# RMS norms of a two-layer hybrid block: squares on two engines, column sums in four column groups, and the inverse root worked out token by token

## The chip, the cores and the metric

The kernel runs on one core of a Trainium2 chip. Every time is device time in microseconds (us) of one launch, and the number to be predicted is its median over several runs. An engine is named as the profile names it: PE is TensorE's matmul, PEld its weight load, ACT ScalarE, DVE VectorE, POOL GpSimd, SP the engine that issues most DMAs.

## The reference, cut to what matters

```python
def rms_norm(x, g):
    xf = x.astype(jnp.float32)
    y = xf * lax.rsqrt(jnp.mean(xf * xf, axis=-1, keepdims=True) + RMS_EPS)
    return (y * g.astype(jnp.float32)).astype(x.dtype)

def modulate(h, shift, scale):
    return h * (1.0 + scale) + shift
...
for layer in range(DEPTH):                    # DEPTH = 2
    hc = modulate(rms_norm(cs, g_norm1), ...)   # 256 context tokens x 1024
    hx = modulate(rms_norm(x, g_norm1), ...)    # 256 latent tokens x 1024
    ... three mixers of h @ w_in, merged and projected: x_mid, c_mid ...
    hx2 = modulate(rms_norm(x_mid, g_norm2), ...)
    x_new = x_mid + gate * swiglu(hx2, w_ffn_in, w_ffn_out)
    # the context half of the second part is left out in the last layer
```

So there are four norms over the stream: three over 512 tokens (context and latent), and the last over the 256 latent tokens alone. Each ends in a large matrix product.

## The kernel before

The stream `X` lies in SBUF transposed: 128 partitions, `DT` = 8 tiles of channels (k), `TOK` = 512 tokens along the free axis. A norm must therefore sum squares across partitions and over the eight tiles, for each token.

The program is a row of stages. Each is one block in which every engine has its own instruction list and waits on counted signals; at a stage's end all engines meet, so nothing of the next stage starts earlier. In a stage each engine works strictly in the written order. `norm` is such a stage, called four times.

In it, in order of the work:

- ACT squares the eight tiles of `X` into `sq` (L614). Then it makes the high parts of the first three chunks of the next stage's weights (`high_ahead`, L615, the instruction is L327; 128x1024 each): weights are cut into a high and a low part so that three fp32r products give nearly an fp32 one.
- PE adds the squares up with a matrix of ones as weights, one fp32 product of 128x512 for each tile, all into bank 0 (L628). An fp32 product shows as two matmul records, so eight products are 16 records. Since `ones` is 128x128, every partition of bank 0 gets the sum.
- DVE makes the three low parts (`low_ahead`, L644, the instruction is L330), then waits for the sums, scales them and adds epsilon (L646, 128x512), and takes the reciprocal (L648, 128x512). ACT takes the square root (L617, 128x512). `rms` holds the inverse root for each token on all partitions.
- Then come the cells: one cell is one channel tile by one segment of 256 tokens, 16 cells in a norm over 512 tokens and 8 in the last. For each, DVE multiplies `X`, a scale and `rms` (L656), ACT adds the shift and rounds to the high part (L621), and the low part is made three cells later by DVE (L663) or, for every third cell, by POOL in two steps (L673, L675).
- PE waits for both segments of a channel tile and multiplies them with the first two weight tiles of the next stage (`AHEAD_TILES` = 2): six fp32r products for each k, 48 in all, into banks 0 and 1 (or 0 and 2). They are the last work of the stage.

In the two norms that open a layer SP also stores the result to DRAM at the end (`save`). The weight ring's first three loads for the next stage are issued in the stage before the norm.

Of the kernel before, what the change touches and what calls it, by code (L numbers as in the profile page):

```python
# [22 lines left out]
ACT = mybir.ActivationFunctionType  # L23
ALU = mybir.AluOpType
AX = mybir.AxisListType

P = 128
D = 1024
DT = D // P
SEQ = 256  # L30
CTX = 256
TOK = CTX + SEQ
# [26 lines left out]
RMS_EPS = 1e-6  # L59
# [9 lines left out]
CHUNKS = 3  # L69
# [110 lines left out]
def build_in(ctx, nc, ins, out):  # L180
    def sb(name, shape):
        return ctx.enter_context(nc.sbuf_tensor(name, shape, FP32))

    def sig(name):
        return Signal(ctx, nc, name)


    X = sb("X", [P, DT, TOK])
    ident = sb("ident", [P, P])
    ones = sb("ones", [P, P])  # L190
# [21 lines left out]
    BANK = ctx.enter_context(nc.psum_tensor("BANK", [P, 8, 512], FP32))  # L212
# [20 lines left out]
    WORK = place("WORK", WORK0, WORK_N)  # L233
# [3 lines left out]
    def carve(mem, at, *shape):  # L237
        n = 1
        for s in shape:
            n *= s  # L240
        flat = mem[:, at:at + n]
        if len(shape) == 1:
            return flat
        names = "abcd"[:len(shape)]
        return flat.rearrange(f"p ({' '.join(names)}) -> p {' '.join(names)}",
                              **{k: s for k, s in zip(names[1:], shape[1:])})
# [131 lines left out]
    pe_sig, act_sig, dve_sig, pool_sig = sig("pe_step"), sig("act_step"), sig("dve_step"), sig("pool_step")  # L378
    rows_turned = sig("rows_turned")
    turned_out = sig("turned_out")  # L380
    squares = sig("squares")
    sums = sig("sums")
    inverse_rms = sig("inverse_rms")
    scaled = sig("scaled")
# [6 lines left out]
    high_ready = sig("weights_high")  # L391
# [23 lines left out]
    class Modulation:  # L415
# [28 lines left out]
        def sums(self, a):  # L444

            return BANK[:, self.turned_bank, 32 * self.supers[a]:32 * (self.supers[a] + 1)]
# [157 lines left out]
    def norm(scale, shift, t0, ahead, banks, save=False):  # L604
        n = TOK - t0
        sq = carve(WORK, 0, DT, TOK)
        rms = carve(WORK, DT * TOK, TOK)
        segs = [s for s in range(2) if s * CTX >= t0]
        cells = [(k, s) for k in range(DT) for s in segs]
        with stage() as block:  # L610
            @block.scalar
            def _(act):
                for k in range(DT):
                    squares.mark(nc.scalar.activation(sq[:, k, t0:], X[:, k, t0:], ACT.Square))  # L614
                ahead.high_ahead(act)  # L615
                act.wait_ge(*dve_sig(2))
                inverse_rms.mark(nc.scalar.activation(rms[:, t0:], rms[:, t0:], ACT.Sqrt))  # L617
                for i, (k, s) in enumerate(cells):
                    a, b = s * CTX, (s + 1) * CTX
                    act.wait_ge(*scaled(i + 1))  # L620
                    gate_ready.mark(nc.scalar.activation(HS[0][:, k, a:b], sq[:, k, a:b], ACT.Identity, bias=shift[:, k, s:s + 1]))  # L621


            @block.tensor
            def _(pe):
                for k in range(DT):
                    pe.wait_ge(*squares(k + 1))
                    last = nc.tensor.matmul(BANK[:, 0, 0:n], ones[:], sq[:, k, t0:], start=(k == 0), stop=(k == DT - 1))  # L628
                sums.mark(last)

                weights = [(ahead.part(0, c), ahead.part(1, c)) for c in range(AHEAD_TILES)]
                pe.wait_ge(*low_ready(AHEAD_TILES))
                for k in range(DT):
                    i = len(segs) * (k + 1)
                    pe.wait_ge(*gate_ready(i))
                    pe.wait_ge(*h_ready(i - i // 3))
                    if i // 3:
                        pe.wait_ge(*evacuated(i // 3))
                    for w, bank in zip(weights, banks):
                        product3(BANK[:, bank, 0:n], [x[:, k] for x in w], [x[:, k, t0:] for x in HS], k == 0, k == DT - 1)  # L640

            @block.vector
            def _(dve):
                ahead.low_ahead(dve)  # L644
                dve.wait_ge(*sums(1))
                dve_sig.mark(nc.vector.tensor_scalar(rms[:, t0:], BANK[:, 0, 0:n], 1.0 / D, RMS_EPS, ALU.mult, ALU.add))  # L646
                dve.wait_ge(*dve_sig(1))
                dve_sig.mark(nc.vector.reciprocal(rms[:, t0:], rms[:, t0:]))  # L648
                dve.wait_ge(*inverse_rms(1))
                LAG = 3  # L650
                lows = [i for i in range(len(cells)) if i % 3 != 2]
                for i in range(len(cells) + LAG):
                    if i < len(cells):
                        k, s = cells[i]
                        a, b = s * CTX, (s + 1) * CTX
                        scaled.mark(nc.vector.scalar_tensor_tensor(sq[:, k, a:b], X[:, k, a:b], scale[:, k, s:s + 1],  # L656
                                                                   rms[:, a:b], ALU.mult, ALU.mult))
                    if i >= LAG and i - LAG in lows:

                        k, s = cells[i - LAG]  # L660
                        a, b = s * CTX, (s + 1) * CTX
                        dve.wait_ge(*gate_ready(i - LAG + 1))
                        h_ready.mark(nc.vector.scalar_tensor_tensor(HS[1][:, k, a:b], sq[:, k, a:b], shift[:, k, s:s + 1],  # L663
                                                                    HS[0][:, k, a:b].bitcast(FP32), ALU.add, ALU.subtract))

            @block.gpsimd
            def _(pool):
                for i, (k, s) in enumerate(cells):
                    if i % 3 == 2:

                        a, b = s * CTX, (s + 1) * CTX
                        pool.wait_ge(*gate_ready(i + 1))
                        pool_sig.mark(nc.gpsimd.tensor_scalar(sq[:, k, a:b], sq[:, k, a:b], shift[:, k, s:s + 1], None, ALU.add))  # L673
                        pool.wait_ge(*pool_sig(i // 3 + 1))
                        evacuated.mark(nc.gpsimd.tensor_tensor(HS[1][:, k, a:b], sq[:, k, a:b], HS[0][:, k, a:b].bitcast(FP32), ALU.subtract))  # L675

            @block.sync
            def _(sp):
                if save:

                    sp.wait_ge(*h_ready(len(cells) - len(cells) // 3))
                    sp.wait_ge(*evacuated(len(cells) // 3))
                    for x in range(2):
                        sp.dma_start(H_DRAM[x], HS[x].bitcast(FP32).rearrange("p k t -> p (k t)")).then_inc(h_saved, 16)
        ahead.early = CHUNKS
        Signal.end_stage()
# [1534 lines left out]
    for l in range(DEPTH):  # L2221
        t0 = CTX if l == DEPTH - 1 else 0
# [61 lines left out]
```

## Time and profile before

| what | value |
|---|---|
| median of 3 runs | 2302.93 us (2298.18 to 2304.2) |
| the profiled execution | 2312.29 us |
| its span (first to last instruction) | 2310.5 us |
| mean granted TensorE clock | 0.940 of full speed |
| PE busy | 2027.9 us (88%) |
| DVE busy | 1071.6 us (46%) |
| ACT busy | 775.8 us (34%) |
| POOL busy | 299.9 us (13%) |

The profiled execution is longer than its span by 1.8 us, and 9.4 us above the median of the runs. The busy shares are means over stages that have different limits; for a change to one kind of stage, only that stage's own timeline tells what bounds it. The granted clock is given as a share of 2.4 GHz: 1.00 is that, 0.50 is 1.2 GHz.

### The profile page before, as it was taken

The numbers are of one execution on the slowest core, as the hardware profiler recorded it, in microseconds if no ns is written. First come the engines' busy times: TensorE is split into PE (matmuls) and PEld (weight loads), VectorE is DVE, ScalarE is ACT, GpSimd is POOL, SyncE is SP. The second block draws the span as 40 slices with busy tenths as digits, with TensorE's granted clock in tenths as the row PEclk, the third lists the DMA queues.
The fourth block names the chain that finished last, engine by engine and source line by source line (L and its number), as shares of the span: only waits on it lengthen the run. The fifth ranks groups of instructions, "written<-read, shape, count | busy, mean of one in ns | idle before, by whom it ended". The sixth has DMA issues, their size and how long they took to land. (4 is left out here: it accounts for less than half of the span.)

```text
span 2310.5 us, 51557 instructions
## 1 busy us (share of the span) xinstructions
PE 2027.9 (88%) x22759; PEld 1596.8 (69%) x22759; DVE 1071.6 (46%) x1753; ACT 775.8 (34%) x1419; POOL 299.9 (13%) x380
## 2 busy tenths in 40 slices
PE   4886888879989998989998998968886998988998
PEld 2662877643567887678886665737775457988988
DVE  1635666652643333353332216476666254545544
ACT  1433333223432222232221114253332343434432
POOL 1102333202000111010001001043331110100000
PEclk8997999989989999999999998979998999999999
DMA  7416000120111332223326753100003012654543
GB/s 269 146 64 237 5 4 5 37 108 1 37 58 62 102 92 83 73 76 107 102 81 235 281 172 123 33 1 4 4 5 123 21 37 94 183 166 135 184 152 123
DMA packets 144606, 220.75 MB, mean 96 GB/s; under 512 B 6846, under 2 KB 123800, under 8 KB 137216
## 3 DMA queue, kind: packets, MB, share of 16 engines
q1 hardware_dynamic: 142880, 215.74, 27.5%
q8 instruction: 181, 2.97, 0.5%
q0 software_dynamic: 1504, 1.71, 0.2%
q14 instruction: 41, 0.34, 0.0%
HBM read 208.00 MB, written 9.44 MB: 94 GB/s over the span
## 5 line engine op out<-in xcount | busy, mean ns | idle before, releaser
L366 PE MATMUL BANK<-H_high,W_high 128*128 128x512 f32 (+2 forms) x1472 | 524.3, 356 | 70.8 <-ACT H_high L621 32.3
L330 DVE TENSOR_TENSOR W_low<-RING,W_high 128x1024 fp32r<-128x1024 f32 x268 | 328.0, 1232 | 466.6 <-ACT W_high L327 466.5
L367 PE MATMUL BANK<-H_low,W_high 128*128 128x512 f32 (+2 forms) x1472 | 519.5, 353 | 0.0
L368 PE MATMUL BANK<-H_high,W_low 128*128 128x512 f32 (+2 forms) x1472 | 518.9, 353 | 0.0
L327 ACT ACTIVATE W_high<-RING 128x1024 fp32r<-128x1024 f32 x268 | 279.2, 1052 | 618.1 <-PE BANK L368 585.1
L366 PEld LDWEIGHTS BANK<-H_high,W_high 128*128 128x128 f32 (+1 forms) x1472 | 283.7, 193 | 118.0 <-issue 50.7
L367 PEld LDWEIGHTS BANK<-H_low,W_high 128*128 128x128 f32 (+1 forms) x1472 | 284.1, 193 | 37.8 <-issue 1.1
L368 PEld LDWEIGHTS BANK<-H_high,W_low 128*128 128x128 f32 (+1 forms) x1472 | 283.3, 192 | 37.7
L1231 PE MATMUL BANK<-RING,WORK 64*64 64x64 f32 x4480 | 177.6, 225 | 11.4 <-issue 6.1
L1231 PEld LDWEIGHTS BANK<-RING,WORK 64*64 64x64 f32 x4480 | 154.4, 137 | 25.3 <-issue 9.3
L1042 POOL TENSOR_TENSOR WORK<-WORK,masks 128x256 f32<-128x256 f32 x160 | 122.8, 781 | 250.5 <-ACT WORK L1083 151.6
L1231 PE MATMUL BANK<-WORK,RING 64*64 64x64 f32 x3072 | 133.6, 232 | 15.5 <-issue 12.7
L366 PE MATMUL BANK<-hidden_high,W_high 128*128 128x512 f32 (+1 forms) x352 | 123.3, 350 | 12.0 <-PEq L2051 12.0
L1231 PE MATMUL BANK<-RING 64*64 64x64 f32 (+1 forms) x2944 | 102.3, 257 | 30.3 <-DVE RING L1137 20.9
L1231 PEld LDWEIGHTS BANK<-WORK,RING 64*64 64x64 f32 x3072 | 112.8, 142 | 20.5 <-issue 16.6
L367 PE MATMUL BANK<-hidden_low,W_high 128*128 128x512 f32 (+1 forms) x352 | 120.9, 343 | 0.0
L368 PE MATMUL BANK<-hidden_high,W_low 128*128 128x512 f32 (+1 forms) x352 | 120.8, 343 | 0.0
L1231 PEld LDWEIGHTS BANK<-RING 64*64 64x64 f32 x2944 | 94.9, 150 | 33.9 <-issue 31.4
L1172 DVE TENSOR_TENSOR RING<-RING,BANK 128x512 f32<-128x512 f32 x128 | 83.8, 684 | 62.6 <-PE BANK L1231 60.4
L1091 ACT ACTIVATE WORK<-BANK 128x256 f32<-128x256 f32 (+1 forms) x160 | 58.0, 363 | 119.3 <-PE BANK L1231 105.3
L1989 POOL TENSOR_TENSOR merge_tiles<-merge_tiles 128x512 f32<-128x512 f32 (+1 forms) x32 | 33.7, 1063 | 481.7 <-DVE merge_tiles L1971 481.7
L366 PEld LDWEIGHTS BANK<-hidden_high,W_high 128*128 128x128 f32 x352 | 68.0, 193 | 34.8 <-issue 27.7
(270 smaller groups left out, 2904.3 us busy)
## 6 DMA issues: line engine op xcount, KB each, us to landing
modulation_weights<-w_mod_dram SPq DMA_DIRECT2D x48, 1024.0 KB, 6.5
RING<-w_in_dram SPq DMA_DIRECT2D x46, 1024.0 KB, 5.7
RING<-w_ffn_in_dram SPq DMA_DIRECT2D x44, 1024.0 KB, 5.2
RING<-w_ffn_out_dram SPq DMA_DIRECT2D x20, 1024.0 KB, 5.5
RING<-w_out_dram SPq DMA_DIRECT2D x8, 1024.0 KB, 5.3
h_high<-H_high SPq DMA_DIRECT2D x2, 2048.0 KB, 6.5
h_low<-H_low SPq DMA_DIRECT2D x2, 2048.0 KB, 12.6
H_high<-h_high SPq DMA_DIRECT2D x2, 2048.0 KB, 12.2
```

Of the source, the lines that this page charges most:

```text
L327: high_ready.mark(nc.scalar.activation(self.part(0, c), self.raw(c), ACT.Copy))
L330: low_ready.mark(nc.vector.tensor_tensor(self.part(1, c), self.raw(c), self.part(0, c).bitcast(FP32), ALU.subtract))
L366: nc.tensor.matmul(out, w[0], x[0], start=start, stop=False)
L367: nc.tensor.matmul(out, w[0], x[1], start=False, stop=False)
L368: return nc.tensor.matmul(out, w[1], x[0], start=False, stop=stop)
L1042: s_lm[d].mark(nc.gpsimd.tensor_tensor(LM[d], LTS[d], lanes(level_mask(d, l)), ALU.mult))
L1091: s_x1_out[d].mark(nc.scalar.activation(X1[d][:, :, cols], pairs(4 * d + B_L, 0)[:, :, cols], ACT.Copy))
L1172: s_t[d].mark(nc.vector.tensor_tensor(T2[d].rearrange("p q j t -> p q (j t)"), T2[d].rearrange("p q j t -> p q (j t)"), BANK[:, 4 * d + B_ ...
L1231: last[x] = nc.tensor.matmul(BANK[to[h], bank, at + j * width:at + (j + 1) * width], lhs(j)[rows[h]], rhs(j)[rows[h]], start=start and (j ...
L1989: pool_sig.mark(nc.gpsimd.tensor_tensor(total(m), total(m), gate(u), ALU.add))
```

## The change

The squares of the even tiles stay on ACT, those of the odd tiles go to DVE. PE adds tile k into column group k mod 4 of bank 0, with weights of only 32 columns: four groups of 32 partitions, each holding the sum of two tiles. ACT copies that bank to SBUF (`partial`). PE then multiplies each block of 128 tokens of `partial`, as weights, with one column of ones: token by token, 128 partitions by 4 columns (2 in the last norm), in bank 6. DVE scales and inverts these 128x4 numbers, ACT takes their root, and PE spreads them back: weights are a column of `by_token` repeated 128 times, the moving matrix is the unit matrix, and the result, the inverse root of every token on all partitions, is left in bank 7. The cells read it there.

The making of the three weight parts ahead is spread between these steps: ACT makes the first high part after its squares, the second after the copy, the third after the root; DVE makes the first low part before the sums by token, the second and third after the reciprocal, and only then waits for bank 7.

```diff
-        rms = carve(WORK, DT * TOK, TOK)
+        partial = carve(WORK, DT * TOK, TOK)
+        by_token = carve(WORK, (DT + 1) * TOK, 4)
+        T_BANK, R_BANK = 6, 7
+        own = slice(t0 // P, TOK // P)
+        tiles = range(t0 // P, TOK // P)
...
             def _(act):
-                for k in range(DT):
+                for k in range(0, DT, 2):
                     squares.mark(nc.scalar.activation(sq[:, k, t0:], X[:, k, t0:], ACT.Square))
-                ahead.high_ahead(act)
+                ahead.make_high(act, 0)
+                act.wait_ge(*sums(1))
+                partial_kept.mark(nc.scalar.activation(partial[:, t0:], BANK[:, 0, 0:n], ACT.Copy))
+                ahead.make_high(act, 1)
                 act.wait_ge(*dve_sig(2))
-                inverse_rms.mark(nc.scalar.activation(rms[:, t0:], rms[:, t0:], ACT.Sqrt))
+                inverse_rms.mark(nc.scalar.activation(by_token[:, own], by_token[:, own], ACT.Sqrt))
+                ahead.make_high(act, 2)
...
             def _(pe):
                 for k in range(DT):
-                    pe.wait_ge(*squares(k + 1))
-                    last = nc.tensor.matmul(BANK[:, 0, 0:n], ones[:], sq[:, k, t0:], start=(k == 0), stop=(k == DT - 1))
+                    pe.wait_ge(*(odd_squares if k % 2 else squares)(k // 2 + 1))
+                    c = k % 4
+                    last = nc.tensor.matmul(BANK[32 * c:32 * (c + 1), 0, 0:n], ones[:, 0:32], sq[:, k, t0:], start=(k < 4), stop=(k >= DT - 4))
+                sums.mark(last)
+                pe.wait_ge(*partial_kept(1))
+                for t in tiles:
+                    last = nc.tensor.matmul(BANK[:, T_BANK, t:t + 1], partial[:, t * P:(t + 1) * P], ones[:, 0:1], start=True, stop=True)
+                sums.mark(last)
+                pe.wait_ge(*inverse_rms(1))
+                for t in tiles:
+                    last = nc.tensor.matmul(BANK[:, R_BANK, t * P:(t + 1) * P], by_token[:, t:t + 1].to_broadcast([P, P]), ident[:], start=True, stop=True)
                 sums.mark(last)
...
             def _(dve):
-                ahead.low_ahead(dve)
-                dve.wait_ge(*sums(1))
-                dve_sig.mark(nc.vector.tensor_scalar(rms[:, t0:], BANK[:, 0, 0:n], 1.0 / D, RMS_EPS, ALU.mult, ALU.add))
+                for k in range(1, DT, 2):
+                    odd_squares.mark(nc.vector.tensor_tensor(sq[:, k, t0:], X[:, k, t0:], X[:, k, t0:], ALU.mult))
+                dve.wait_ge(*high_ready(1))
+                ahead.make_low(0)
+                dve.wait_ge(*sums(2))
+                dve_sig.mark(nc.vector.tensor_scalar(by_token[:, own], BANK[:, T_BANK, own], 1.0 / (32 * D), RMS_EPS, ALU.mult, ALU.add))
                 dve.wait_ge(*dve_sig(1))
-                dve_sig.mark(nc.vector.reciprocal(rms[:, t0:], rms[:, t0:]))
-                dve.wait_ge(*inverse_rms(1))
+                dve_sig.mark(nc.vector.reciprocal(by_token[:, own], by_token[:, own]))
+                for c in range(1, CHUNKS):
+                    dve.wait_ge(*high_ready(c + 1))
+                    ahead.make_low(c)
+                dve.wait_ge(*sums(3))
...
                         scaled.mark(nc.vector.scalar_tensor_tensor(sq[:, k, a:b], X[:, k, a:b], scale[:, k, s:s + 1],
-                                                                   rms[:, a:b], ALU.mult, ALU.mult))
+                                                                   BANK[:, R_BANK, a:b], ALU.mult, ALU.mult))
```

## Rows read from the trace of the kernel before

**Rows 1.** The page, part 1: busy time, share, instructions of each engine.

```profile
PE 2027.9 (88%) x22759; PEld 1596.8 (69%) x22759; DVE 1071.6 (46%) x1753; ACT 775.8 (34%) x1419; POOL 299.9 (13%) x380
```

**Rows 2.** Timeline, first norm: start, duration (us), engine, line, operation, [idle before <-releaser].

```profile
54.03 4.26 ACT L614 ACTIVATE WORK<-X 128x512 f32<-128x512 f32 x8 [11.39 <-PEq L537]
...
58.20 2.93 ACT L327 ACTIVATE W_high<-RING 128x1024 fp32r<-128x1024 f32 x3
...
59.27 3.50 DVE L330 TENSOR_TENSOR W_low<-RING,W_high 128x1024 fp32r<-128x1024 f32 x3 [14.06 <-ACT W_high L327]
...
61.15 1.28 ACT L617 ACT_TABLE_LOAD   x1
...
63.35 0.69 DVE L646 TENSOR_SCALAR WORK<-BANK 128x512 f32<-128x512 f32 x1 [0.58 <-PE BANK L628]
64.08 3.35 DVE L648 RECIPROCAL WORK<-WORK 128x512 f32<-128x512 f32 x1
67.46 0.63 ACT L617 ACTIVATE WORK<-WORK 128x512 f32<-128x512 f32 x1 [5.03 <-DVE WORK L648]
68.13 1.67 DVE L656 SCALAR_TENSOR_TENSOR WORK<-X,scale,WORK 128x256 f32<-128x256 f32 x4 [0.70 <-ACT WORK L617]
```

**Rows 3.** Timeline of PE: the column sums of the first, second and last norm.

```profile
54.71 8.60 PE L628 MATMUL BANK<-WORK,ones 128*128 128x512 f32 x16 [10.15 <-ACT WORK L614]
...
972.84 7.13 PE L628 MATMUL BANK<-WORK,ones 128*128 128x512 f32 x16 [1.89 <-ACT WORK L614]
...
2089.57 3.72 PE L628 MATMUL BANK<-WORK,ones 128*128 128x256 f32 x16 [1.29 <-ACT WORK L614]
```

**Rows 4.** Timelines of ACT and DVE, second and last norm: first square, first cell.

```profile
972.15 4.26 ACT L614 ACTIVATE WORK<-X 128x512 f32<-128x512 f32 x8 [16.84 <-PEq L2007]
...
985.58 1.67 DVE L656 SCALAR_TENSOR_TENSOR WORK<-X,scale,WORK 128x256 f32<-128x256 f32 x4 [0.70 <-ACT WORK L617]
...
2089.10 2.56 ACT L614 ACTIVATE WORK<-X 128x256 f32<-128x256 f32 x8 [8.36 <-PEq L2007]
...
2098.73 1.68 DVE L656 SCALAR_TENSOR_TENSOR WORK<-X,scale,WORK 128x256 f32<-128x256 f32 x4 [0.48 <-ACT WORK L617]
```

**Rows 5.** Timeline of PE, first norm: first and last product of the tiles ahead.

```profile
71.27 0.77 PE L366 MATMUL BANK<-H_high,W_high 128*128 128x512 f32 x1 [7.96 <-ACT H_high L621]
...
84.07 0.39 PE L368 MATMUL BANK<-H_high,W_low 128*128 128x512 f32 x1
```

**Rows 6.** Stretches of the first norm: length, PE, PEld, DVE, ACT, POOL busy, PEclk, DMA.

```profile
54.00:58.00 4.00, 3.29 (x4) 1.50 (x5) 0.00 (x0) 3.97 (x8) 0.00 (x0) 0.54 0.00 0
...
71.00:75.00 4.00, 3.73 (x9) 3.00 (x10) 4.00 (x8) 1.93 (x5) 2.81 (x4) 0.53 0.00 0
```

**Rows 7.** Timeline of PE: products in four column groups of 32, elsewhere in the kernel.

```profile
31.27 1.06 PE L440 MATMUL BANK<-modulation_weights,condition_padded 128*32 128x512 f32 x8
...
37.50 1.94 PE L440 MATMUL BANK<-modulation_weights,condition_padded 128*32 128x512 f32 x8 [3.45 <-DMA modulation_weights<-w_mod_dram]
```

**Rows 8.** Timeline of PE: short fp32 products with 128x128 weights.

```profile
26.78 4.55 PE L574 MATMUL BANK<-ident,WORK 128*128 128x128 f32 x24
...
1391.32 1.03 PE L456 MATMUL BANK<-ident,modulation_rows 128*128 128x8 f32 x8 [0.76 <-DVE mod L479]
1392.72 1.85 PE L456 MATMUL BANK<-ident,modulation_rows 128*128 128x8 f32 x8 [0.38 <-DVE mod L479]
```

**Rows 9.** Groups by form: xcount | busy us, mean ns of one | idle before.

```profile
L656 DVE SCALAR_TENSOR_TENSOR WORK<-X,scale,WORK 128x256 f32<-128x256 f32 x56 | 28.0, 536 | 2.6 <-ACT WORK L617 2.6
...
L663 DVE SCALAR_TENSOR_TENSOR H_low<-WORK,mod,H_high 128x256 fp32r<-128x256 f32 x39 | 24.2, 636 | 0.0
...
L1997 DVE SCALAR_TENSOR_TENSOR X<-BANK,mod,X 128x256 f32<-128x256 f32 x48 | 20.6, 479 | 68.2 <-PE BANK L368 68.2
...
L1759 DVE RECIPROCAL WORK<-WORK 128x1 f32<-128x1 f32 x48 | 7.4, 154 | 0.9 <-ACT WORK L1787 0.2
...
L1105 ACT ACTIVATE decay<-WORK 128x4 f32<-128x4 f32 x32 | 6.3, 196 | 0.0
```

More of the change, by code:

```diff
@@ L380, in build_in @@
     turned_out = sig("turned_out")
-    squares = sig("squares")
+    squares, odd_squares, partial_kept = sig("squares"), sig("squares_of_odd_tiles"), sig("partial_sums_kept")
     sums = sig("sums")
```

## The prediction

> **What bounds the kernel now.** I read the page first: PE is busy 88% of the span [rows 1], so most stages are bound by products. That says nothing of a norm, so I read the timeline of each one. In the first, ACT's first square starts at 54.03 and DVE's first cell at 68.13: 14.1 us in which no cell is made [rows 2]. The reader should follow who ends last at each step. ACT's eight squares are over by 58.3, but PE adds them up one after another until 63.31 [rows 2, 3]; DVE has made its three low parts by 62.8 and waits 0.58 us for PE; then scale (0.69), reciprocal (3.35) and root (0.63) follow one upon the other, with no other engine at work [rows 2]. From first square to first cell I read 14.10 us in the first norm, 13.43 in the second, 9.63 in the last [rows 2, 4]; the third norm repeats the first (14.08). In the second norm PE ends its sums at 979.97, earlier than in the first because its clock is high, and there DVE's low parts end last. After the first cell PE needs 3.14 us to its first product ahead and ends 16.33 us after the first cell [rows 2, 5]. All engines meet at a stage's end, and PE ends a norm, so what is saved in front of the first cell moves everything behind it. The weight loads ahead had landed: ACT went from its squares into the high parts with no gap [rows 2].
>
> **The change, part by part.** I set time 0 at the first square and write s for the end of the sums.
>
> Squares. Eight on ACT took 4.26 us, so they start 0.52 apart and four end at 2.2 [rows 2]. On DVE three two-input operations of 1024 columns took 3.50 us, so I take 0.6 for one of 512 [rows 2] and four end near 2.6. Both halves run side by side.
>
> Sums. 16 records in four column groups are what the modulation does: eight records (four groups, two records each, 512 columns) take 1.06 us at the full clock and 1.94 at the half clock [rows 7], where 16 records of the present form take 7.13 and 8.60 [rows 3]. So four products cost about one. The last square is ready at 2.7; at the full clock its product ends one product later, s = 3.7. In the first and third norm PE starts at the half clock (0.54 over the first 4 us, [rows 6]): a group's second product waits for its first (0.7 to 2.4, 1.5 to 3.2), and the last ends at 5.05 if the clock stays low, 4.4 if it rises as soon as it did before. I take s = 4.7. In the last norm products are half as long: s = 2.1.
>
> From the sums to the cells. ACT has by then squared and made the first high part (2.2 + 1.0, a third of 2.93, [rows 2]). Then on ACT: copy of the bank, 0.63 as its root of the same size; second high part 0.98; table load for the root 1.28, which stands behind that high part and ahead of the root, as it stood ahead of the wait before; root of 128x4, 0.2 [rows 2, 9]; third high part 1.06. DVE makes the third low part (1.2) only then, and the cells are written behind it. Beside this runs the other branch: the products by token, eight records of weights 128x128, like a turn of the modulation at 1.03 or, at the half clock, 1.85 us [rows 8]; scale and reciprocal of four columns, near 0.2 each ([rows 9]: 0.154 for one column). It ends at s + 0.7 + 1.9 + 0.5 = s + 3.1 at the half clock against s + 2.9 for the table load, so the two branches nearly tie. The spreading products are eight records of 128 columns: at 0.19 each [rows 8] 1.5 us, 1.9 with their hand-overs; they start when the root is there, and lie beside the third high and low part, 2.3 us: hidden, with a few tenths to spare. If they took 1 us more, each norm would lose about 0.7. So the first cell comes at s + 5.35 with a full clock, s + 5.6 with a half.
>
> That gives 10.3 for the first and third norm (before 14.10 and 14.08: 3.8 saved in each), 9.05 for the second (13.43: 4.4 saved). In the last norm ACT is not held up by the sums: 1.24 squares, 0.98 high, 0.31 copy, 0.98 high, 1.3 table, 0.2 root, 1.06 high, 1.2 low with hand-overs, 7.3 (9.63: 2.3 saved). Sum 14.3 us. Removed with it are three reciprocals of 3.35 and one of 1.75; they are inside this sum, not on top of it.
>
> The cells. They are written as before, but the inverse root is read from PSUM. A like operation with one PSUM operand takes 479 ns on average, the present one 536, and its shortest was 471 [rows 9]. So a cell costs no more, and the excess of the two SBUF forms over 475 ns (56 x 61 ns and 39 x 161 ns, 9.7 us over four norms) is what DVE loses while POOL works beside it; if the first form is freed of it, DVE gains up to 3.4 us, perhaps more if POOL then meets it less often. How much of this reaches the stage's end is set by PE: in the first norm 48 products took 12.8 us [rows 5] after a start at 0.53 of the clock [rows 6]; at 0.43 each while low for 3.3 us and 0.229 after, they need 12.5 from their start, so only 0.6 is to be had there and in the third norm, 0.2 in the second (there PE hardly waited) and nothing in the last. I take 1.5 in all; the bounds are 0, and 2.2 for each long norm and 2.4 for the last if PE's products also found the full clock.
>
> A rule of the Trainium skill bears on this: SBUF — State Buffer, "Who interferes with whom", says that a DVE instruction with at most one SBUF input does not contend with GpSimd, one with two such inputs does. By that rule the trace's 536 would fall to 475 in the new form; no row here shows this form beside a busy POOL. Another speaks against the change: TensorEngine Tiling (Array Packing), "Key Properties", says that a change of tiling mode drains TensorE. The trace shows no gap of that kind (the turns of X end at 31.33, the grouped products begin at 31.27, [rows 7, 8]); even an emptied pipe twice a norm, estimated at the 0.2 by which one record outlasts its turn, would be 1.6 us in all, and 14.2 would be saved.
>
> Sum: 14.3 + 1.5 = 15.8 us. Against the profiled execution (2312.3, span 2310.5) that is 2296.5; this execution lay 9.4 above the median, and I carry the difference over: 2302.9 - 15.8 = 2287.1. No other stage changes; no DMA is added or moved.
>
> **The rivals.**
> 1. The products find the clock high. PE's last work before them is now the spreading, about 4 us earlier, not 8. If the clock holds, the cells set the pace, freed of POOL: 14.3 + 3 x 2.2 + 2.4 = 23.3 saved, 2279.6. Against it: the turns at 1391 to 1394 are such short bursts, and the third of them ran at the half clock, 1.85 instead of 1.03 [rows 8]. Chance 0.15.
> 2. The hand-overs cost more. The chain now crosses engines six times, and the table load, the third high and the third low part stand in line. If the products with repeated weights or the small steps need 2 us more in each norm, 8 is lost: 2295. For it: little slack; against: every piece has a like row. Chance 0.14.
> 3. The groups don't overlap, since a wait now stands ahead of each product. Then s is as before (9.3, 7.8, 9.3, 4.2), the first cells come at 14.8, 13.2, 14.8 and 9.5, and 2304 is the time. Against it: while a group works the next squares are already there, and in the modulation eight grouped records took 1.06 us where half of the 16 serial ones take 3.6 [rows 3, 7]. Chance 0.05.
> 4. Slower: reading PSUM on DVE while PE writes to other banks. 56 cells take one such operand each. From 0.28 us more for a cell it eats 15.8; at twice the 0.4 by which cells now follow each other it costs 22.4, 2309.5. Against it: the 479 ns are of an operation that ran while PE wrote. Chance 0.03.
>
> **How the numbers follow.** The forecast, 2287.1, gets 0.63. Its own range is 2283 to 2291: s of the first and third norm (0.7 either way), the tie of the branches (0.3 a norm), the cells (0 to 3) and the runs' own scatter (3 us each way). The range of 8 in 10 reaches down to most of the first rival and up to the second: 2279 to 2295. A change under 0.3% (6.9 us) can't be told from none here. Faster than that: the forecast, rival 1 and somewhat over half of rival 2, 0.86. Slower: rival 4, 0.03. Same: 0.11.
>
> **What would show it.** In the profile after: column sums with 128*32 weights ending 3.7 after the first square in the second norm and 4.4 to 5.1 in the first; a table load between the second high part and a root of 128x4; the third low part right ahead of the first cell, at 10.3, 9.05, 10.3 and 7.3; the cell's mean near 475 to 480 ns; PE's last product about 15.7 after the first cell. Wrong would be: sums of 7 us; DVE idle ahead of the first cell with PE as releaser (then the spreading is not hidden); a table load more for a norm; cells over 0.6 us.

## The result, and the profile after

The changed kernel takes 2286.54 us (median of 6 runs, 2279.83 to 2289.74), the kernel before 2303.56 us over the 6 runs beside it (2298.18 to 2311.22). The ratio is 0.9917, with a 95% interval of 0.9900 to 0.9935. Forecast were 2287.1, in a range of 2279 to 2295. When both were run again on another occasion, the ratio was 0.994 (0.992 to 0.996); the two intervals meet between 0.992 and 0.9935, 15 to 18 us.

The timeline of the changed kernel's first norm answers to [rows 2]; lines are start, duration, engine, line, operation, and the idle time before with its releaser.

```profile
52.42 2.19 ACT L618 ACTIVATE WORK<-X 128x512 f32<-128x512 f32 x4 [10.25 <-PEq L537]
52.45 2.50 DVE L662 TENSOR_TENSOR WORK<-X 128x512 f32<-128x512 f32 x4 [7.70 <-PEq L537]
53.10 4.02 PE L637 MATMUL BANK<-WORK,ones 128*32 128x512 f32 x16 [9.01 <-ACT WORK L618]
54.52 1.04 ACT L327 ACTIVATE W_high<-RING 128x1024 fp32r<-128x1024 f32 x1
...
57.17 0.60 ACT L621 ACTIVATE WORK<-BANK 128x512 f32<-128x512 f32 x1 [1.61 <-PE BANK L637]
57.66 1.05 ACT L327 ACTIVATE W_high<-RING 128x1024 fp32r<-128x1024 f32 x1
57.82 1.05 PE L641 MATMUL BANK<-ones,WORK 128*128 128x1 f32 x8 [0.69 <-ACT WORK L621]
58.73 1.28 ACT L624 ACT_TABLE_LOAD   x1
58.91 0.16 DVE L666 TENSOR_SCALAR WORK<-BANK 128x4 f32<-128x4 f32 x1 [2.09 <-PE BANK L641]
59.10 0.18 DVE L668 RECIPROCAL WORK<-WORK 128x4 f32<-128x4 f32 x1
...
60.02 0.21 ACT L624 ACTIVATE WORK<-WORK 128x4 f32<-128x4 f32 x1
60.13 1.04 ACT L327 ACTIVATE W_high<-RING 128x1024 fp32r<-128x1024 f32 x1
60.28 2.07 PE L645 MATMUL BANK<-ident,WORK 128*128 128x128 f32 x8 [1.41 <-ACT WORK L624]
61.20 1.23 DVE L330 TENSOR_TENSOR W_low<-RING,W_high 128x1024 fp32r<-128x1024 f32 x1 [0.81 <-ACT W_high L327]
62.39 1.66 DVE L679 SCALAR_TENSOR_TENSOR WORK<-X,scale,BANK 128x256 f32<-128x256 f32 x4
...
65.38 0.76 PE L366 MATMUL BANK<-H_high,W_high 128*128 128x512 f32 x1 [3.02 <-ACT H_high L629]
...
78.47 0.39 PE L368 MATMUL BANK<-H_high,W_low 128*128 128x512 f32 x1
```

The reader should see two chains that meet. The sums end at 57.12, 4.70 after the first square; ACT's copy, PE's products by token and DVE's two small steps end at 59.28; but the root starts at 60.02, since the table load stands in front of it on ACT. From there one branch goes through PE's spreading (ends 62.35), the other through the third high and the third low part (ends 62.43, and the first cell starts 0.04 before that). Then PE waits 3.02 us for the first channel tile.

Read in the same way in every norm, this gives the following table (us). The last product's end less the first square's start is a norm's time.

| norm | sums end, before / after | first cell, before / after | first cell to last product, before / after | norm, before / after |
|---|---|---|---|---|
| first | 9.28 / 4.70 | 14.10 / 9.97 | 16.33 / 16.47 | 30.43 / 26.44 |
| second | 7.82 / 3.63 | 13.43 / 8.84 | 16.34 / 16.75 | 29.77 / 25.59 |
| third | 9.27 / 4.63 | 14.08 / 9.89 | 16.36 / 16.44 | 30.44 / 26.33 |
| last | 4.19 / 2.13 | 9.63 / 7.13 | 10.29 / 9.82 | 19.92 / 16.95 |
| all | | 51.24 / 35.83 | | 110.56 / 95.31 |

So the four norms gained 15.25 us: 15.41 in front of the first cell, and behind it they lost 0.16. In the groups by form the cells and DVE's low parts are quicker, as [rows 9] let one hope:

```profile
L679 DVE SCALAR_TENSOR_TENSOR WORK<-X,scale,BANK 128x256 f32<-128x256 f32 x56 | 24.6, 478 | 0.0
L686 DVE SCALAR_TENSOR_TENSOR H_low<-WORK,mod,H_high 128x256 fp32r<-128x256 f32 x39 | 18.6, 494 | 0.0
```

478 and 494 ns stand against 536 and 636. Why the norm does not end earlier for it is seen in the stretches of the first norm (columns as in [rows 6]):

```profile
60.00:65.00 5.00, 2.07 (x8) 1.78 (x8) 4.19 (x9) 3.00 (x8) 0.68 (x1) 0.51 0.00 0
65.00:70.00 5.00, 4.62 (x11) 3.68 (x12) 5.00 (x14) 3.61 (x8) 4.32 (x6) 0.50 0.00 0
```

PE's clock stands at 0.50, 1.2 GHz, for the first 5.0 us of the products ahead (until 70.37), and PE has no gap in them. PE ended the norm before the change too, but there the products ran at the half clock for 3.5 us only (71.27 to 74.77).

**Why the two spans differ by 28.** The profiled spans are 2310.5 and 2282.5, and only 15.25 of the 28.0 lie in the norms. Of the other 12.8, half (6.4) lies in the two scan stages. The marks at the ends of the features and scan stages, with first and last start (first and second layer), show it. Before, then changed, then the kernel before in another execution:

```profile
L762 POOLq EVENT_SEMAPHORE  x4: 17/17/17, 221.4 to 1538.3; - x4
...
L1023 POOLq EVENT_SEMAPHORE  x4: 17/17/17, 454.7 to 1762.7; - x4
```

```profile
L785 POOLq EVENT_SEMAPHORE  x4: 17/17/17, 216.0 to 1517.0; - x4
...
L1046 POOLq EVENT_SEMAPHORE  x4: 17/17/17, 444.7 to 1739.6; - x4
```

```profile
L762 POOLq EVENT_SEMAPHORE  x4: 17/17/17, 221.1 to 1530.6; - x4
...
L1023 POOLq EVENT_SEMAPHORE  x4: 17/17/17, 447.1 to 1751.1; - x4
```

The two scans took 233.3 + 224.4 = 457.7 before, 228.7 + 222.6 = 451.3 changed, and 226.0 + 220.5 = 446.5 in the kernel before run again, which is less than in the changed one. So the scans differ by that much without any change; for the remaining 6.4 us outside the scans I have no stage to name. A single trace of each is thus good for the norms and not for the sum.

### The profile page after: what moved, and what is told of

It reads as the page before. It is cut to its first block and busy times, and to the rows that moved or that the text cites. A ratio compares the mean times of both kernels' runs of the same rounds, so it can differ in the third digit from the quotient of the medians.

```text
span 2282.5 us, 51673 instructions
## 1 busy us (share of the span) xinstructions
PE 2014.0 (88%) x22815; PEld 1591.9 (70%) x22815; DVE 1059.4 (46%) x1769; ACT 767.9 (34%) x1407; POOL 298.2 (13%) x380
## 3 DMA queue, kind: packets, MB, share of 16 engines
q0 software_dynamic: 1504, 1.71, 0.2%
## 5 line engine op out<-in xcount | busy, mean ns | idle before, releaser
L1254 PEld LDWEIGHTS BANK<-RING,WORK 64*64 64x64 f32 x4480 | 153.8, 135 | 30.1 <-issue 12.8
L1254 PE MATMUL BANK<-WORK,RING 64*64 64x64 f32 x3072 | 127.8, 226 | 11.8 <-issue 9.1
L1254 PEld LDWEIGHTS BANK<-WORK,RING 64*64 64x64 f32 x3072 | 107.0, 137 | 16.4 <-issue 12.1
L1254 PEld LDWEIGHTS BANK<-RING 64*64 64x64 f32 x2944 | 90.8, 145 | 32.5 <-issue 30.3
## 6 DMA issues: line engine op xcount, KB each, us to landing
h_low<-H_low SPq DMA_DIRECT2D x2, 2048.0 KB, 12.8
```

The lines of the kernel that those rows point to most:

```text
L1254: last[x] = nc.tensor.matmul(BANK[to[h], bank, at + j * width:at + (j + 1) * width], lhs(j)[rows[h]], rhs(j)[rows[h]], start=start and (j ...
```

## The experiments

Each is an edit of the changed kernel unless it says otherwise; ratios are to the kernel before, on the same chip, with a 95% interval behind. "Norms" is the time of the four norms together in the run's trace (110.56 before, 95.31 changed), and first cells are counted from the first square.

**1. Column groups undone.**

```diff
-    last = nc.tensor.matmul(BANK[32 * c:32 * (c + 1), 0, 0:n], ones[:, 0:32], sq[:, k, t0:], start=(k < 4), stop=(k >= DT - 4))
+    last = nc.tensor.matmul(BANK[:, 0, 0:n], ones[:], sq[:, k, t0:], start=(k == 0), stop=(k == DT - 1))
...
-    1.0 / (32 * D)
+    1.0 / (P * D)
```

> The changed kernel, but the column sums with the whole 128-column matrix of ones again (all into bank 0, one product after another; the mean's divisor becomes 128 x D, since each partition then holds the whole sum). Theory (the gain is all in front of the first cell and hangs on when the sums end): the sums end 9.3, 7.8, 9.3 and 4.2 us after the first square again, instead of 4.70, 3.63, 4.6 and 2.1; the first cell comes 4.6, 4.2, 4.6 and 2.2 later than in the changed kernel (14.5, 13.0, 14.5, 9.4 after the first square), 15.6 in all, so that nothing is left of the change: ratio to the kernel before 0.998 to 1.002. Rival (the gain is the removed 128x512 reciprocals and roots): those stay removed, so at least 10 us of the gain stays, ratio 0.995 or less.

Measured: 0.9999 (0.9982 to 1.0016). In PE's timeline of the second norm:

```profile
968.72 7.13 PE L637 MATMUL BANK<-WORK,ones 128*128 128x512 f32 x16 [1.89 <-ACT WORK L618]
976.54 1.05 PE L641 MATMUL BANK<-ones,WORK 128*128 128x1 f32 x8 [0.69 <-ACT WORK L621]
```

The sums take 7.13 again instead of 2.94, the first cells come at 14.69, 13.08, 14.56 and 9.20, and the norms take 109.9 together. All but 0.7 us of the gain is gone, though the wide reciprocals and roots stay removed. ACT's timeline in the same norm shows why:

```profile
975.89 0.60 ACT L621 ACTIVATE WORK<-BANK 128x512 f32<-128x512 f32 x1 [4.72 <-PE BANK L637]
976.38 1.05 ACT L327 ACTIVATE W_high<-RING 128x1024 fp32r<-128x1024 f32 x1
977.45 1.28 ACT L624 ACT_TABLE_LOAD   x1
```

ACT stands idle for 4.72 us beside the sums, and only then come copy, second high part, table load, root, third high and third low part. From the sums' end to the first cell it is 5.2 to 5.3 us in the long norms, where the kernel before needed 4.8 to 5.6 with its wide reciprocal, since it had made the weight parts beside the sums. So the sums' end sets the chain in the new order; narrow steps with the parts made beside late sums were not run.

**2. Squares on ACT alone.**

```diff
-    for k in range(0, DT, 2):
+    for k in range(DT):
         squares.mark(nc.scalar.activation(sq[:, k, t0:], X[:, k, t0:], ACT.Square))
...
-    for k in range(1, DT, 2):
-        odd_squares.mark(nc.vector.tensor_tensor(sq[:, k, t0:], X[:, k, t0:], X[:, k, t0:], ALU.mult))
```

> The changed kernel with all eight squares on ACT and none on DVE. Theory: the last square ends 4.3 us after the first starts instead of 2.5, the sums end 1.0 to 1.7 later (5.3 in the second norm, 5.6 to 5.9 in the first and third, 3.1 in the last) and the first cell as much: +1.1, +1.7, +1.1, +1.2, about 5 us lost of the change's 15 to 17; ratio to the kernel before 0.994 to 0.996. Rival (the engines' split of the squares does not matter because PE's groups are still adding): under 1 us lost.

Measured: 0.9946 (0.9928 to 0.9964), norms 98.5. The sums end at 5.36 in all three long norms and 3.23 in the last, since ACT's 4.26 us now set them (5.6 to 5.9 was expected in the first and third); the first cells come 0.66, 1.74, 0.69 and 1.22 later. Of the 4.3 us lost there 1.1 came back behind the first cell, where the long norms' products ran at the half clock for 3.7 to 4.2 us instead of 4.9 to 5.6. The split of the squares is worth 3.2 us in the traces; the interval overlaps that of the changed kernel.

**3. Mean, reciprocal and root 128x512 wide.**

```diff
-    for t in tiles:
-        last = nc.tensor.matmul(BANK[:, T_BANK, t:t + 1], partial[:, t * P:(t + 1) * P], ones[:, 0:1], start=True, stop=True)
+    sums.mark(nc.tensor.matmul(BANK[:, T_BANK, 0:n], ones[:], partial[:, t0:], start=True, stop=True))
...
-    dve_sig.mark(nc.vector.reciprocal(by_token[:, own], by_token[:, own]))
+    dve_sig.mark(nc.vector.reciprocal(rms[:, t0:], rms[:, t0:]))
...
-    BANK[:, R_BANK, a:b], ALU.mult, ALU.mult))
+    rms[:, a:b], ALU.mult, ALU.mult))
```

> The changed kernel, but the partial sums are added by one 128x512 product with the matrix of ones, and mean, reciprocal and root are again made 128x512 wide in SBUF, from where the cells read them (no work token by token, no spreading product). Squares and column groups stay. Theory: from the end of the sums to the first cell 8.9 us instead of 5.2 (0.7 copy, 1.1 product, 0.7, 3.35, 0.7, then the third high and low part), so 3.7 lost in each norm over 512 tokens and near 2 in the last, 13 in all; DVE's cells go back to 536 ns mean beside POOL, but as PE's 48 products bound the stage this costs no more than 0.5 a norm. Ratio to the kernel before 0.997 to 1.000. Rival (the cells' relief from POOL is worth something at the stage's end): the time from first cell to last product grows by 1.5 us or more in a norm over 512 tokens, ratio over 1.001.

Measured: 0.9973 (0.9961 to 0.9985), norms 108.2. The second norm's timeline:

```profile
977.58 3.35 DVE L662 RECIPROCAL WORK<-WORK 128x512 f32<-128x512 f32 x1
...
980.97 0.63 ACT L624 ACTIVATE WORK<-WORK 128x512 f32<-128x512 f32 x1 [3.09 <-DVE WORK L662]
...
983.72 1.67 DVE L673 SCALAR_TENSOR_TENSOR WORK<-X,scale,WORK 128x256 f32<-128x256 f32 x4
```

From the sums' end to the first cell it is 8.7 us, not 5.2; first cells 13.71, 12.34, 13.28 and 8.23. Behind the first cell 16.77, 16.76, 16.48 and 10.65, against 16.47, 16.75, 16.44 and 9.82: the rival's 1.5 us a norm is not there. With the column groups and without the narrow steps only 2.3 of the 15.25 us are left in the norms. The runs came out 6 us faster than before (3.5 to 9); the trace's 2.3 lies below that interval, and I name no cause for it.

**4. The cells read from SBUF.**

```diff
+    act.wait_ge(*sums(3))
+    partial_kept.mark(nc.scalar.activation(rms[:, t0:], BANK[:, R_BANK, t0:], ACT.Copy))
...
-    BANK[:, R_BANK, a:b], ALU.mult, ALU.mult))
+    rms[:, a:b], ALU.mult, ALU.mult))
```

> The changed kernel with one more step: ACT copies the spread inverse root from bank 7 to SBUF and the cells read it there, as before the change. Theory: DVE's cells and low parts are again slowed beside POOL (means near 536 and 636 ns instead of 477 and 484, the pair of cells 1.35 instead of 0.87), yet the time from first cell to PE's last product stays at 16.5 (within 0.5), since the products bound it; the copy itself delays the first cell by 0.7, 0.4, 0.7 and 0. Sum +1 to +3 us against the changed kernel. Rival (the PSUM operand is worth 2 us a norm): +6 us or more, with the time from first cell to last product 18 or more.

Measured: 0.9941 (0.9921 to 0.9962), norms 97.15, that is 1.84 more. The groups by form, and a pair of cells in DVE's timeline:

```profile
L682 DVE SCALAR_TENSOR_TENSOR WORK<-X,scale,WORK 128x256 f32<-128x256 f32 x56 | 28.0, 536 | 1.6 <-ACT WORK L628 1.6
L689 DVE SCALAR_TENSOR_TENSOR H_low<-WORK,mod,H_high 128x256 fp32r<-128x256 f32 x39 | 24.2, 636 | 0.0
```

```profile
981.83 1.35 DVE L682 SCALAR_TENSOR_TENSOR WORK<-X,scale,WORK 128x256 f32<-128x256 f32 x2
```

536 and 636 ns are back to the last digit, so it was the PSUM operand that had freed DVE of POOL. The totals behind the first cell hardly differ: 16.97, 16.52, 16.34 and 9.54, against 16.47, 16.75, 16.44 and 9.82, 0.1 less in all. But the clock differs too: here the products ran at the half clock for 5.7, 4.7, 3.9 and 3.1 us (17.4 in all), in the changed kernel for 5.0, 5.6, 4.9 and 3.7 (19.2).

**5. The changed kernel again.**

> The changed kernel once more, with more rounds. The four norms took 15.25 us less in its trace than in that of the kernel before, while the medians differ by 17.0 and the two spans by 28. Theory (only the norms changed; the rest is how single executions differ, above all in the scan stages): the difference of the medians comes to 13 to 18 us, ratio 0.9920 to 0.9945, and the norms again take 95 to 96 us together. Rival (the scan or another stage gained too): a steady 20 us or more, ratio under 0.9915.

Measured: 0.994 (0.992 to 0.996), 14.1 us between the medians; norms 95.7. As the first theory has it. Its two scans took 225.7 + 215.8 = 441.5, 10 less than in the first trace of the same kernel.

**6. PE kept busy in front of the products ahead.** Six products that compute nothing of use:

```diff
     sums.mark(last)          # behind the spreading products
+    pe.wait_ge(*high_ready(1))
+    for _ in range(6):
+        nc.tensor.matmul(BANK[:, WARM_BANK, 0:TOK], ahead.part(0, 0).rearrange("p k w -> p (k w)")[:, 0:P], WS2[0][:, 0, 0:TOK], start=True, stop=True)
```

> The changed kernel with six products on PE that compute nothing of use (128x512 fp32r, into the unused bank 5), issued between the spreading products and the products ahead, where PE stands idle for 3 us. Theory (behind the first cell the stage is bound by PE's 48 products, of which the first run at the half clock because PE was nearly idle before them): the clock is up when the products start or within 1 us of it, the time from first cell to last product falls from 16.5 to 14.0 to 14.7 in the norms over 512 tokens and from 9.8 to 8 to 8.5 in the last, the norms take 86 to 89 us together instead of 95.3: 6 to 9 us faster than the changed kernel, ratio to the kernel before 0.989 to 0.991. Rival (the tail is bound by the cells, POOL's last low part, and a high clock only lets PE wait): from first cell to last product not under 16, under 2 us faster.

Measured: 0.9921 (0.9902 to 0.9941), norms 88.1. PE's timeline in the first norm, and its stretches (all engines, clock third from the end):

```profile
59.68 1.49 PE L645 MATMUL BANK<-ident,WORK 128*128 128x128 f32 x8 [1.41 <-ACT WORK L624]
60.82 2.91 PE L649 MATMUL BANK<-W_high 128*128 128x512 f32 x6
64.73 0.47 PE L366 MATMUL BANK<-H_high,W_high 128*128 128x512 f32 x1 [1.00 <-ACT H_high L629]
```

```profile
62.00:64.00 2.00, 1.73 (x5) 0.81 (x3) 2.00 (x6) 1.71 (x4) 0.33 (x1) 0.56 0.00 0
64.00:66.00 2.00, 1.27 (x6) 1.08 (x7) 2.00 (x6) 1.42 (x3) 1.72 (x3) 1.00 0.00 0
```

The clock is at 1.00 when the products start, and from first cell to last product it takes 14.20, 14.22 and 14.23 in the long norms. In the last norm it was 9.70, not 8 to 8.5: its products started at the full clock after a gap of 2.16 us, and 0.7 us later the clock fell for 3.4 us. The norms are 7.2 us shorter than in the changed kernel's first trace, as expected; the medians' ratio moved by 0.002 (4 us) from that of the changed kernel run beside it, less than expected, and the two intervals overlap.

**7. Such products in every gap of PE**: two behind the sums, four behind the products by token, eight behind the spreading.

> As the run before this one, but such products stand in all three gaps of PE: two behind the column sums, four behind the products by token, eight behind the spreading products. Theory: PE's clock, once up, stays up through the norm; the spreading products take 1.1 instead of 2.1. The first cell stays where DVE's third low part puts it, or comes up to 1 us later where the four products still run at the half clock ahead of the spreading (1.7 us in a gap of 1.4). From first cell to last product 14.0 to 14.5. Within 2 us of the run before this one, either way. Rival (what is issued in front of a waiting product delays the chain more than the clock gives back): 2 us or more slower than the run before this one.

Measured: 0.9914 (0.9892 to 0.9936), norms 88.5. The last norm now keeps its clock (8.71 behind the first cell), but the third loses it in the middle of its products:

```profile
1384.66 2.10 PE L653 MATMUL BANK<-W_high 128*128 128x512 f32 x8
1388.79 0.47 PE L366 MATMUL BANK<-H_high,W_high 128*128 128x512 f32 x1 [2.03 <-ACT H_high L629]
...
1390.02 0.59 PE L368 MATMUL BANK<-H_high,W_low 128*128 128x512 f32 x1
```

```profile
1387.00:1390.00 3.00, 1.21 (x5) 1.05 (x6) 3.00 (x9) 2.45 (x6) 1.99 (x3) 1.00 0.00 0
1390.00:1393.00 3.00, 3.00 (x9) 2.29 (x8) 3.00 (x9) 1.92 (x4) 2.62 (x4) 0.51 0.00 0
```

At the full clock the eight products end 2.03 us before the first product ahead; the clock drops at about 1390 while PE is busy again, and that norm needs 15.75 behind the first cell. Yet the first norm had the same gap, and there the clock held through all 48 products:

```profile
63.84 0.47 PE L366 MATMUL BANK<-H_high,W_high 128*128 128x512 f32 x1 [2.05 <-ACT H_high L629]
```

```profile
64.00:75.00 11.00, 11.00 (x48) 8.66 (x47) 7.70 (x20) 5.17 (x11) 7.56 (x9) 1.00 0.17 70
```

So it did in the second (gap 2.04); both need 14.19. With gaps of 0.9 to 1.2 us (experiment 6) the clock held in all three long norms; at 2 us it held twice and fell once, and what decided between them is not shown.

**8. The third high and low part behind the cells.**

```diff
-    ahead.make_high(act, 2)
     for i, (k, s) in enumerate(cells):
...
+    ahead.make_high(act, 2)      # behind ACT's cells; likewise the third low part on DVE
```

> The changed kernel with the third high part at the end of ACT's list and the third low part at the end of DVE's, behind the cells, so that the cells wait for the spreading products alone. Theory (the branch through the third parts and the spreading products tie): nothing gained in the first and third norm, where the spreading ends 0.04 ahead of the first cell at the half clock, 0.2 in the second, 1.2 in the last, 1.4 us in all, and the third parts are hidden behind PE's products. Rival (the third parts alone hold the cells up): 1.0 to 2.3 us a norm, 5 us or more in all.

Measured: 0.9934 (0.9911 to 0.9957), norms 94.85. First cells 10.00, 8.56, 9.95 and 5.82. In the last norm PE is now the releaser:

```profile
2066.54 0.71 PE L645 MATMUL BANK<-ident,WORK 128*128 128x128 f32 x4 [1.86 <-ACT WORK L624]
2067.29 1.66 DVE L678 SCALAR_TENSOR_TENSOR WORK<-X,scale,BANK 128x256 f32<-128x256 f32 x4 [0.88 <-PE BANK L645]
```

Only the last norm gains much (1.3 at its first cell; 0.3 in the second); in the first and third the two branches tie as expected.

**9. Experiments 6 and 8 together**, with the fillers of experiment 7 in the last norm alone, and in the two norms where ACT waits longest for the sums the table load drawn into that wait:

```diff
     ahead.make_high(act, 0)
+    if save:
+        nc.scalar.activation(by_token[:, 4:5], ones[:, 0:1], ACT.Sqrt)
```

> The changed kernel with three additions. Third high and low part behind the cells. Six products of no use ahead of the products ahead in the norms over 512 tokens, and two, four and eight in the three gaps of the last norm, where PE's clock stayed up with them. In the two norms that save their result, where ACT waits 1.5 us for the sums, one root of a constant right behind the first high part, so that the table is loaded in that wait. Theory: first cell 0.6 earlier than 9.9 to 10.0 in the first and third norm (9.3), 8.6 in the second, 5.8 in the last; from first cell to last product 14.2, 14.2, 14.2 and 8.5; the norms together 85 to 86 us instead of 95.3, so 9 to 10 us faster than the changed kernel and 24 to 25 faster than the kernel before, ratio 0.988 to 0.991. Rival (the clock's rise is not held when the chain is shorter, or the load of the table is only moved): norms at 90 us or more, not faster than the run with six products alone (88.1).

Measured: 0.9914 (0.9894 to 0.9934), norms 86.5. First cells 8.89, 10.15, 8.92 and 5.81; in the second norm PE ran at the half clock for 3.4 us from 968.65 on, while it made the sums, which cost it 1.3 there. Behind the first cell 14.66, 14.65 and 14.65, not 14.2. Who is late is seen in the first norm:

```profile
73.20 1.23 DVE L330 TENSOR_TENSOR W_low<-RING,W_high 128x1024 fp32r<-128x1024 f32 x1 [0.21 <-ACT W_high L327]
73.25 1.77 POOL L708 TENSOR_TENSOR H_low<-WORK,H_high 128x256 fp32r<-128x256 f32 x1
...
75.17 0.47 PE L366 MATMUL BANK<-H_high,W_high 128*128 128x512 f32 x1 [0.18 <-POOL H_low L708]
```

POOL's last step began 0.05 after DVE's third low part, both with two inputs in SBUF, and took 1.77 us instead of 0.74; PE waited for it. The norms are 8.8 us shorter than the changed kernel's, a little less than expected; the ratio missed its range (0.988 to 0.991), and its interval overlaps that of the changed kernel.

**10. The kernel before, against itself.**

> The kernel before once more, timed against itself, for what a difference of two executions is worth. Theory (what varies lies outside the norms): ratio 0.998 to 1.002, the norms 110 to 111.5 us together, the two scan stages anything from 441 to 460 us together. Rival: the norms themselves vary by over 3 us, and the 15 us read from two traces are then not safe.

Measured: 1.0006 (0.9991 to 1.0022); norms 111.4, scans 446.5. The norms vary by 0.8 (in the first norm, whose sums took 0.7 longer at the half clock), the scans by 11.

**11. Experiment 9 with the third low part held back.**

```diff
     dve.wait_ge(*high_ready(3))
+    dve.wait_ge(*evacuated(len(cells) // 3))
     ahead.make_low(2)
```

> The combined kernel with one wait more: DVE makes the third low part only when POOL has made its last low part. In the combined kernel POOL's last step took 1.77 us instead of 0.74 in the first norm, since DVE's third low part, with two inputs in SBUF, began 0.05 before it, and PE's last channel tile waited for POOL; from first cell to last product it was 14.65 instead of the 14.2 of the run with six products alone. Theory (the two block each other): POOL's last step is back at 0.74 and the time from first cell to last product at 14.2 in the three long norms, 1.3 us in all, the norms 84 to 85.5 together; on the clock not to be told from the combined kernel, ratio 0.988 to 0.992. Rival (the third low part is now so late that the stage ends by DVE): 14.65 or more as before.

Measured: 0.9874 (0.985 to 0.9897), 2265.48 us against 2295.74. In the first norm:

```profile
72.97 0.73 POOL L709 TENSOR_TENSOR H_low<-WORK,H_high 128x256 fp32r<-128x256 f32 x1
73.81 1.23 DVE L330 TENSOR_TENSOR W_low<-RING,W_high 128x1024 fp32r<-128x1024 f32 x1 [1.10 <-POOL H_low L709]
```

POOL's step is back at 0.73, and behind the first cell it is 14.20, 14.24, 14.22 and 8.73. So the wait was the cause of POOL's long step. The norms take 85.45, that is 25.1 less than before the change, 9.9 less than after it, and 1.0 less than in experiment 9. The runs say more than that: 30.3 us less than the kernel before where experiment 9 had 20.5, and a ratio below the range expected (0.988 to 0.992). The 9 us on top are not in the norms, and no cause is shown for them. This kernel has the lowest ratio of all; its interval lies below those of the changed kernel's two measurements and just meets those of experiments 7 and 9.

## Why the prediction was right, point by point

**The squares and the sums: right.** Forecast were s = 4.7, 3.7 and 2.1; the trace has 4.70, 3.63 and 2.13, with 4.63 in the third norm. The groups do overlap as in [rows 7], with a wait ahead of every product: rival 3 is out. Without this step almost nothing is left (experiment 1), and without the narrow steps 2.3 us (experiment 3): the gain needs both.

**From the sums to the first cell: right in kind, 0.2 to 0.4 us a norm too long.** I had 10.3, 9.05, 10.3 and 7.3; it was 9.97, 8.84, 9.89 and 7.13. In the first and third norm I priced the products by token at the half clock, 1.85; they found the full one, 1.05. So the small steps were over 0.74 ahead of the root, and the table load held it, where I had expected a near tie. The spreading in turn ran at the half clock (2.07, forecast 1.9) and did tie with the third high and low part, as forecast; experiment 8 confirms it, since with those parts out of the way the first and third norm gained nothing at their first cell, and in the last PE became the releaser. The gain in front of the first cell is 15.4, not 14.3. Rival 2 (hand-overs that cost 2 us more) is out.

**The cells: the wrong term.** The working of the cells said that of DVE's relief 1.5 us would reach the stages' ends. The relief came in full (478 and 494 ns), and experiment 4 ties it to the PSUM operand; but the term measured -0.16 in the trace of the change and -0.1 by experiment 4. The mis-sized piece is the 3.3 us for which I let PE's products run at the half clock. By the granted clock it was 3.5, 4.2, 3.5 and 4.7 in the four norms before (16.0 us in all, and 16.7 when the kernel before ran again) and 5.0, 5.6, 4.9 and 3.7 in the changed kernel (19.2, and 19.8 when it ran again). A product starts every 0.43 us at the half clock and every 0.23 at the full one, so 1 us at the half clock costs 0.46, and the 3.2 us more cost 1.5 by this estimate. The relief itself was then worth about 1.3 us, near the forecast; corrected in the same way, experiment 4 gives 0.7. The longer time at the half clock took it back. The sum behind the 0.6 a norm was loose as well: the 12.8 us count from the first product's start to the last one's start, the 12.5 all 48 products; on one footing it is 12.8 against 12.3.

**Rival 1 as a counterfactual.** I gave it 0.15 and 14.15 us behind the first cell. It did not happen, but experiment 6 made it happen in the long norms, and then it took 14.20 to 14.23. It is not the cells that set the pace there, as I had it: PE's 48 products start within 10.8 us, 0.23 each, with hardly a wait among them. So what bounds a long norm behind its first cell is the number of products at the clock's level. Work on PE in front of them raised that level, but the length of the gap alone does not decide it (experiment 7). The forecast of that rival's last norm, 7.9, was too low: 8.7.

**Rival 4** is out: the cells' 478 ns were measured while PE wrote to other banks.

**The skill's rules.** The traces agree with the rule of the Trainium skill, SBUF — State Buffer, "Who interferes with whom": 536 ns with two SBUF inputs and 478 with one, POOL being busy beside both. It says too that the order of issue, not the shape, decides who blocks, and experiment 9 agrees: POOL's step took 1.77 behind a DVE instruction that began 0.05 earlier. The other rule, that a change of tiling mode drains TensorE (TensorEngine Tiling (Array Packing), "Key Properties"), leaves no mark that could be seen here: in the second norm the sums ended where the forecast without it had them, within 0.07, and the products by token follow the sums after 0.69 us, with the change of mode as without it (experiment 1), both times waiting for ACT's copy.

**The total.** 14.3 + 1.5 = 15.8 was forecast, 15.25 is in the trace, and 17.0 and 14.1 are in the two measurements. Two errors nearly cancel in it: 1.1 too little in front of the first cell, 1.7 too much behind it. The median's nearness to the forecast (0.6 us) is luck beyond that: the six runs of the changed kernel spread over 10 us, and what the two spans differ by outside the norms (12.8) would have misled anyone who read the gain from them.

## What to carry to other kernels

Column groups of 32 pay where a product's rows are all alike: eight 512-wide fp32 sums took 2.94 instead of 7.13 us, and every step behind them moved up by as much. Work on one number per token costs far less on 128x4 than on 128x512 (0.18 against 3.35 us for a reciprocal). But ask what else stands in the line: here two high parts, the table load and a low part had moved behind the sums, so that either half of the change alone gained 0.7 or 2.3 us in the norms, and both together 15.25. Before the work behind such a chain is made quicker, ask at which clock the closing products will start; and where DVE and POOL both end a stage, see that their two-input instructions do not meet.

## What the runs showed of the hardware that was not expected

The clock did not only fall while PE was idle. In experiment 7 it dropped at 1390 when PE had been busy again for over 1 us, after a gap of 2.03 us, and in the last norm of experiment 6 0.7 us after the products had begun, behind a gap of 2.16; behind gaps of 2.05, 2.04 and 1.71 us in experiment 7 it held. Short bursts (1.05 us by token, 2.07 us spreading) did not keep it up in any long norm of the changed kernel. In the first norm it fell at 60.1, in the 1.4 us of idleness ahead of the spreading products:

```profile
58.90:60.10 1.20, 0.00 (x0) 0.00 (x0) 1.16 (x3) 1.19 (x2) 0.00 (x0) 1.00 0.00 0
60.20:62.30 2.10, 2.02 (x8) 1.78 (x8) 1.29 (x2) 0.97 (x2) 0.00 (x0) 0.50 0.00 0
```

In the second norm it fell when these had run for 0.4 us. And in the long norms the products ahead ran longer at the half clock after the change (4.9 to 5.6 us) than before it (3.5 to 4.2), though PE's gap in front of them was shorter (3.0 to 3.3 us instead of 8 to 8.8). Why that is so was not settled.
